# The first projection step as eight plain products, and an earlier load of the second step's weights

## The reference, cut to what matters

```python
def hybrid_layer(hid, norm_pre_w, w_in, ...):
    u = rms_norm(hid, norm_pre_w)                        # (2048, 1024)
    proj = jnp.einsum('bsd,de->bse', u, w_in)            # 6672 columns
    q, k, v, g_attn, z, xbc, dt_raw = jnp.split(proj, ...)
    attn = mixture_of_dilations(q, k, v) * silu(g_attn)
    y = ssd_chunked(silu(conv(xbc)), softplus(dt_raw + dt_bias), ...)   # and its gate and norm
    out = einsum(concat(attn, y), w_out)
    return hid + rms_norm(out, norm_post_w)
```

## Time and profile before

| | |
|---|---|
| time, median of 3 runs | 2194.11 us (2193.91 to 2195.1) |
| the profiled execution's own time | 2193.86 us |
| its span, first to last instruction | 2192.1 us |
| PE busy | 2131.7 us, 97% |
| opening (to the copy of dt's second part) | 0 to 54.78 us |
| steps 0 to 3, with the rounds | 54.87 to 136.55 us |

### The profile page before, as it was taken

The page is one execution under the profiler, slowest core; times in us unless marked ns, Lnnn a source line. Parts: engine busy times, 40 slices in busy tenths (PEclk is TensorE's granted clock), DMA queues, the critical chain, the costliest instruction groups (busy, mean ns, idle before and its releaser), DMA issues.

```text
span 2192.1 us, 34748 instructions
## 1 busy us (share of the span) xinstructions
PE 2131.7 (97%) x12009; PEld 1824.1 (83%) x12009; DVE 1374.5 (63%) x2581; ACT 1039.6 (47%) x2412; POOL 1443.0 (66%) x877
## 2 busy tenths in 40 slices
PE   6999999999999999999999999999997999999998
PEld 4778888888888887888889999999996788888877
DVE  7656666444556665363477777777777866766662
ACT  5334444343433443344357777777775622332231
POOL 5778888777678987777845564655642555655552
PEclk9999999999999999999999999999998899999999
DMA  4552333333623333343375656556547444434431
GB/s 152 198 182 88 111 109 116 115 97 122 224 94 99 96 125 106 109 122 97 115 168 127 155 135 145 120 146 155 135 110 250 153 140 145 139 125 135 135 104 58
DMA packets 261564, 288.23 MB, mean 131 GB/s; under 512 B 78516, under 2 KB 229232, under 8 KB 253328
## 3 DMA queue, kind: packets, MB, share of 16 engines
q1 hardware_dynamic: 260384, 278.68, 43.1%
q0 software_dynamic: 1008, 7.34, 0.8%
HBM read 195.80 MB, written 81.53 MB: 127 GB/s over the span
## 4 chain that ended last, share of the span: by engine, by line
PE 87%; DVE 4%; issue 3%; ACT 3%; DMA 2%; POOL 1%; SPq 0%; DVEq 0%; POOLq 0%; ACTq 0%
PE mm L1124 14%; PE mm L1126 14%; PE mm L1125 14%; PE ps_o L1885 9%; PE ps_t L1872 5%; PE ps_out L2481 5%; PE ps_out L2482 5%; PE ps_out L2488 5%; PE ps_s L1864 4%; PE ps_s L1865 3%; PE ps_y L2523 2%; PE turn L1226 2%; PE ps_state L2513 1%; PE ps_y L2504 1%; DMA tok_tile<-in_x_dram 1%
## 5 line engine op out<-in xcount | busy, mean ns | idle before, releaser
L1124 PE MATMUL mm<-b_hi,w_hi 128*128 128x512 f32 x1456 | 572.3, 393 | 8.3 <-DVE fm L902 6.5
L1126 PE MATMUL mm<-b_hi,w_lo 128*128 128x512 f32 x1456 | 567.9, 390 | 0.0
L1125 PE MATMUL mm<-b_lo,w_hi 128*128 128x512 f32 x1456 | 567.4, 390 | 0.0
L603 POOL TENSOR_TENSOR w_lo<-w_raw,w_hi 128x512 fp32r<-128x512 f32 x208 | 301.3, 1456 | 79.7 <-ACT w_hi L676 72.0
L1124 PEld LDWEIGHTS mm<-b_hi,w_hi 128*128 128x128 f32 x1456 | 273.9, 188 | 66.3 <-issue 10.4
L1126 PEld LDWEIGHTS mm<-b_hi,w_lo 128*128 128x128 f32 x1456 | 273.8, 188 | 57.6
L1125 PEld LDWEIGHTS mm<-b_lo,w_hi 128*128 128x128 f32 x1456 | 274.1, 188 | 55.6
L676 ACT ACTIVATE w_hi<-w_raw 128x512 fp32r<-128x512 f32 x208 | 130.8, 630 | 261.3 <-PE mm L1126 240.8
L1872 PE MATMUL ps_t<-ident_b,probs 128*128 128x128 f32 x1136 | 213.5, 278 | 6.3 <-ACT probs L1797 5.0
L902 DVE SCALAR_TENSOR_TENSOR fm<-mm,u 128x512 f32<-128x512 f32 x120 | 92.3, 769 | 181.9 <-PE mm L1126 181.7
L2481 PE MATMUL ps_out<-wo_hi,mix_hi 128*128 128x512 f32 x480 | 193.9, 404 | 1.3 <-ACT mix_hi L2374 1.3
(11 more groups left out here) (266 smaller groups left out, 4460.9 us busy)
## 6 DMA issues: line engine op xcount, KB each, us to landing
w_raw<-in_w_in_dram SPq DMA_DIRECT2D x52, 1024.0 KB, 5.3
feat<-fm SPq DMA_DIRECT2D x56, 512.0 KB, 5.0
tok<-tok_tile SPq DMA_DIRECT2D x52, 512.0 KB, 3.5
raw_q<-feat SPq DMA_DIRECT2D x32, 512.0 KB, 5.8
raw_k<-feat SPq DMA_DIRECT2D x32, 512.0 KB, 6.4
cum_b<-cum_scratch SPq DMA_DIRECT2D x16, 1024.0 KB, 7.5
cls_nat<-cls_out SPq DMA_DIRECT2D x64, 132.0 KB, 2.7
v_cls<-tok SPq DMA_DIRECT2D x64, 128.0 KB, 4.0
```

The lines of the kernel that those rows point to most:

```text
L603: pool.tensor_tensor(wl[o][:, :, :], source(o, n), wh[o][:, :, :].bitcast(F32), ALU.subtract)\
L1124: pe.matmul(bank, w_hi[:, k, :], bh[o][:, k, :], start=(opens and k == 0), stop=False)
L1125: pe.matmul(bank, w_hi[:, k, :], bl[o][:, k, :], start=False, stop=False)
L1126: last = pe.matmul(bank, w_lo[:, k, :], bh[o][:, k, :], start=False, stop=(closes and k == KH - 1))
```

## The change

Step 0 is no longer done by Strassen's scheme. Its outputs are A11 B11 + A12 B21, A21 B11 + A22 B21, and, since T1 = B12 - B11, A11 B11 + A11 T1 + A12 B22 and A21 B11 + A21 T1 + A22 B22: eight block products in six groups (`first_product`), of which four outputs are read by DVE (`first_read`) with two copies by ACT (`keep_first`). They stand among the transposes of the opening, which are reordered: B22 and T1 of all lanes first, then T3, T2, T4. POOL's block sums and three low parts of step 0 fall away. Of DVE's sums T2 is made in place. Weights of step 1 are loaded right behind the taps, where they used to wait for the last transpose; three tiles move to other rooms, so that this load has its room free. ACT makes the high part of A11 of step 1 ahead of the squares of round 0. Counts of semaphores follow (`products_before` and the like).

```diff
+FIRST_PRODUCTS, FIRST_READS, FIRST_PARTS, FIRST_COPIES = 6, 4, 4, 2
+A21 = S3
...
-        x_rooms = [*x_tok, x_wide[:, 0:D_MODEL], x_wide[:, D_MODEL:2 * D_MODEL]]
+        x_rooms = [*x_tok, place(nc, "x_lane2", SLOT_AT, [P, D_MODEL])[:, :],
+                   place(nc, "x_lane3", W_LO1_AT, [P, D_MODEL])[:, :]]
...
-        START_PARTS += [(o, j) for j in range(LANES) for o in (B22, T1, T3, T2, T4)]
+        START_PARTS += [(o, j) for j in range(LANES) for o in (B22, T1)]
+        START_PARTS += [(o, j) for j in range(LANES) for o in (T3, T2, T4)]
...
+            load_w(1)
             for i in range(HT, HT + 2):
-                sp.wait_ge(u_turned, GROUP_AT + 5 * (i - HT + 1))
+                sp.wait_ge(u_turned, PART_AT[T4, i - HT] + 1)
                 load_x(i)
-            sp.wait_ge(u_turned, START)
-            load_w(1)
...
-            sums(0)
-            low(0, 0)
-            token_sums(0)
+            pool.wait_ge(w_landed[0], 16)
+            low(A11, 0)
+            low(A12, 0)
+            token_sum(T1, 0)
+            low(A21, 0)
+            token_sum(T1, 1)
+            low(A22, 0)
             pool.wait_ge(dt_hi_made, 1)
...
+            def keep_first(o, seen, kept):
+
+                act.wait_ge(product, o)
+                act.activation(kept[:, :], seen[:, :], ACT.Copy, scale=steps[0].scale).then_inc(act_read, 1)
...
+                for r in range(GROUP_AT + 2 * j, GROUP_AT + 2 * j + 2):
+                    token_high(r, START_PARTS[r])
+                if j == 1:
+                    keep_first(1, mm[0], c1)
+                if j == 2:
+                    keep_first(3, mm[2], u2)
+            for j in range(LANES):
+                for r in range(SUMS_AT + 3 * j, SUMS_AT + 3 * j + 3):
                     token_high(r, START_PARTS[r])
                 if j == 0:
-                    high(5, 0)
-                    high(6, 0)
-                    read_first(steps[0])
-            read_dt_early()
+                    read_dt_early(0)
+            read_dt_early(1)
 
             for s in steps:
                 n = s.n
+                if n == 0:
+                    high(0, 1)
                 if n in PREP:
                     for half in range(2):
                         square(HT + 2 * PREP[n] + half)
...
-                for r in range(GROUP_AT + 5 * j, GROUP_AT + 5 * j + 5):
+                for r in range(GROUP_AT + 2 * j, GROUP_AT + 2 * j + 2):
                     token_low(r, START_PARTS[r])
+            first_read(2, 1, put(steps[0], 0, 0), mm[1], c1)
+            for j in range(LANES):
+                token_sums(j)
+                if j == 1:
+                    first_read(4, 2, put(steps[0], 1, 0), mm[0], u2)
+                for r in range(SUMS_AT + 3 * j, SUMS_AT + 3 * j + 3):
+                    token_low(r, START_PARTS[r])
+            first_read(5, 1, put(steps[0], 0, 1), mm[1], c1)
+            first_read(6, 2, put(steps[0], 1, 1), mm[2], u2)
...
                 if n == 0:
                     dve.wait_ge(u_turned, START)
-                else:
-                    dve.wait_ge(dve_read, READS * n)
+                    late_sums(PREP[n])
+                    continue
...
+            def first_product(bank, parts, *pairs):
+
+                pe.wait_ge(lo_made, parts)
+                for i, (w, o) in enumerate(pairs):
+                    last = dozen(bank[:, :], wh[w], wl[w], o, i == 0, i == len(pairs) - 1)
+                last.then_inc(product, 1)
...
             for j in range(LANES):
-                for r in range(GROUP_AT + 5 * j, GROUP_AT + 5 * j + 5):
+                for r in range(GROUP_AT + 2 * j, GROUP_AT + 2 * j + 2):
                     early_rows(r)
-                    if r == GROUP_AT:
-                        multiply(steps[0], 0)
                 if j == 0:
-                    pe.wait_ge(dt_lo_made, 1)
-                    dt_part(dt_banks[0], 0, B11, opens=True)
+                    pe.wait_ge(u_lo_made, GROUP_AT)
+                    first_product(mm[0], 1, (A11, B11))
                 elif j == 1:
-                    dt_part(dt_banks[0], 1, B21, closes=True).then_inc(dt_product, 1)
+                    first_product(mm[1], 2, (A12, B21))
+                    first_product(mm[2], 3, (A21, B11))
                 elif j == 2:
-                    dt_part(dt_banks[1], 0, B11, opens=True)
...
+                    pe.wait_ge(act_read, 1)
+                    first_product(mm[0], 4, (A22, B21))
+            pe.wait_ge(dt_lo_made, 1)
+            dt_part(mm[3], 0, B11, opens=True)
+            dt_part(mm[3], 1, B21, closes=True).then_inc(dt_product, 1)
+            for j in range(LANES):
+                for r in range(SUMS_AT + 3 * j, SUMS_AT + 3 * j + 3):
+                    early_rows(r)
+                if j == 1:
+                    pe.wait_ge(u_lo_made, SUMS_AT)
+                    pe.wait_ge(dve_read, 1)
+                    first_product(mm[1], 4, (A11, T1), (A12, B22))
+                elif j == 2:
+                    pe.wait_ge(act_read, 2)
+                    first_product(mm[2], 4, (A21, T1), (A22, B22))
+            pe.wait_ge(dt_read, 1)
+            dt_part(mm[3], 0, B11, opens=True)
+            dt_part(mm[3], 0, T1)
+            dt_part(mm[3], 1, B22, closes=True).then_inc(dt_product, 1)
...
             for s in steps:
                 n = s.n
-                for o in range(PRODUCTS):
-                    if n or o:
-                        multiply(s, o)
+                for o in range(PRODUCTS if n else 0):
+                    multiply(s, o)
```

More of the change, by code:

```diff
@@ L621, in gpsimd @@
                                dt_w[:, :, 0:SSM_HEADS].bitcast(F32), ALU.subtract).then_inc(dt_lo_made, 1)
[L622 to L631, removed]
+            token_sum(T1, 2)
+            token_sum(T3, 0)
+            token_sum(T1, 3)
+            for j in range(1, LANES):
+                token_sum(T3, j)
             for n in range(1, STEPS):
@@ L671, in high @@
                 act.wait_ge(w_landed[n % 2], 16 * (n // 2 + 1))
[L672 to L675, removed]
+                if n == 1:
+                    if o in (S2, S1, S4):
+                        act.wait_ge(u_turned, START)
+                    else:
+                        act.wait_ge(product, FIRST_PRODUCTS - 1 if o in (A11, A12) else FIRST_PRODUCTS)
+                elif n:
+                    act.wait_ge(product, products_before(n - 1) + o + 1)
+                if n and o in (S1, S2, S3, S4):
+                    act.wait_ge(sums_made, 4 * (n - 1) + {S1: 1, S2: 2, S3: 3, S4: 4}[o])
                 act.activation(wh[o][:, :, :], source(o, n), ACT.Copy).then_inc(hi_made, 1)
@@ L679, in square @@
                 act.wait_ge(rows_in[lane(i)], x_count(i))
-                act.activation(squares[:, :], x_room(i), ACT.Square, accum_out=sum_sq[:, i:i + 1])\
+                squares = u_tok[i] if i < LANES else early_squares if i < HT else half_tanh[:, :]
+                act.activation(squares, x_room(i), ACT.Square, accum_out=sum_sq[:, i:i + 1])\
                    .then_inc(squared, 1)
@@ L744, in reload, with read_dt_early @@
                     op = RELOAD[n, o]
-                    act.wait_ge(product, PRODUCTS * (TURN - 1) + op + 1)
+                    act.wait_ge(product, products_before(TURN - 1) + op + 1)
                     for j in range(LANES):
                         token_high(START + op * LANES + j, (op, j))
[L749 to L753, removed]
+            def read_dt_early(tb):
+                act.wait_ge(dt_product, tb + 1)
+                act.activation(dt_early_out[0:2 * SSM_HEADS, block_cols(tb)], mm[3][0:2 * SSM_HEADS, :], ACT.Copy)\
+                   .then_inc(dt_read, 1)
             def read_dt_late():
@@ L822, in scalar @@
                     read_first(s)
-                high(0, n + 1)
+                if n:
+                    high(0, n + 1)
                 for part in due(n, 0):
@@ L1093, in vector @@
                     cumulate()
[L1094 removed]
+                dve.wait_ge(dve_read, reads_before(n) + 3)
                 if s.conv:
@@ L1611, in gpsimd @@
             pool.memset(early.minus_half[:, :], -0.5).then_inc(S["made"], 1)
-            pool.wait_ge(first.product, PRODUCTS * LAST_STEP + S2 + 1)
+            pool.wait_ge(first.product, products_before(LAST_STEP) + S2 + 1)
             pool.memset(early.state[:, :, :], 0.0).then_inc(S["made"], 1)
```

165 lines of the change are left out of this document (86 added, 79 removed).

## The result

| | before | after |
|---|---|---|
| time, median of 5 runs each | 2194.11 us (2193.54 to 2195.1) | 2204.68 us (2202.88 to 2207.11) |
| the profiled execution's own time | 2193.86 us | 2205.18 us |
| its span | 2192.1 us | 2203.4 us |

The change makes the kernel slower: ratio 1.0048, 95% interval 1.0033 to 1.0063, 10.6 us by the medians. The forecast was 2204.3.

A forecast was written before the change was run, and what follows sets the result against it. The rounds, not PE, were taken to set the pace up to the end of step 3. 2193.86 + 11.5 (longer opening) - 1.1 (shorter round 0) = 2204.3 us, range 2198 to 2209.

The forecast's parts named there:

- Opening: PE before step 1: seven more products, product 1 at half clock and a 2.0 us stall make it 11.5 us longer.
- E: Start of ACT's copy of dt's second part, at the opening's end; forecast at 66.3 instead of 54.8.
- Round 0: ACT and DVE from the copy of dt to the store: 12.9 us instead of 14.0, 1.1 us gained.
- Steps 1 to 3: PE starts step 1 at 68.9, then waits about 12 us ahead of S1 (92.1); S4 at 100.8, not 90.4.
- The sum: Whole kernel: 2193.86 + 11.5 - 1.1 = 2204.3 us; this forecast was given 70%.
- The early load: Step 1's weights loaded ahead of tiles 8 and 9 in SP's queue; said to bring nothing.
- (a): Rival, faster: PE sets the pace, step 1 starts 3.4 us earlier; 2185 to 2190.5 us; chance 8%.
- (b): Rival, no change within 0.2%: opening grows by 5.6 only, round gains 2 or more; 2195 to 2198 us; chance 12%.
- (c): Rival, longer opening: a second half-clock stretch puts the copy of dt at 70 to 72; 2208 to 2210 us; chance 10%.

The follow-up runs named there:

- e4: The changed kernel with the load of step 1's weights put back behind the opening's last transpose; 2206.18 us, ratio 1.0054 to the kernel before.
- e5: The changed kernel with round 0's rows stored twice and SP waiting for both stores before loading round 1's tiles; 2207.23 us, ratio 1.0065.
- e1: The changed kernel with round 0 (squares, normalisations, late sums) moved into the opening; 2190.91 us, ratio 0.9987 to the kernel before.
- e7: e1 with round 0's late sums earlier, round 1's squares early, and step 0's outputs stored right behind the loads of round 1's tiles; 2188.89 us.
- e10: e7 with ACT's high part of A11 of step 1 put ahead of its copy of dt's second part; 2188.54 us, ratio 0.9978.
- e3: The kernel before, without the change, with rounds 0 and 1 moved early; 2188.92 us, ratio 0.9977, and 2187.81 us when run again.
- e11: e10 with SP's load of step 3's weights moved behind the loads of round 2's tiles; 2188.55 us, ratio 0.9978 to the kernel before.
- e2: e1 with round 1 moved early too (its squares and late sums); 2190.54 us, ratio 0.9985 to the kernel before.
- e12: e3 with SP's load of step 3's weights moved behind the loads of round 2's tiles; 2186.43 us, ratio 0.9968 to the kernel before.

## Why the prediction was right

**Opening: right.** Product 1 at 22.46 (22.8), at half clock to 27.73, which is 5.27 (5.1); one stall of 1.90 (2.0), at T2 of lane 1, where it was expected; no other gap up to 66.6; E at 66.69 (66.3), 11.9 behind before's 54.78. PE's timeline of after, beside the earlier trace rows:

```profile
22.46 0.78 PE L1182 MATMUL mm<-b_hi,w_hi 128*128 128x512 f32 x1
27.73 0.62 PE L1242 MATMUL turn<-ident,tok_tile 128*128 128x128 f32 x4
46.14 0.66 PE L1242 MATMUL turn<-ident,tok_tile 128*128 128x128 f32 x4 [1.90 <-DVE tok_tile L919]
69.26 0.80 PE L1182 MATMUL mm<-b_hi,w_hi 128*128 128x512 f32 x1 [2.40 <-POOL w_lo L630]
```

**Round 0: right, one term small.** The store came 12.3 behind E (78.96 less 66.69) for a forecast of 12.9: 1.7 gained, not 1.1. I had counted one normalisation as freed from POOL. Both were, as DVE's timeline of after shows beside the earlier trace rows, which gave 0.7 more. The way from the square to the first normalisation was 0.4 shorter too (67.70 to 69.46), and the four sums, as expected not freed, took 0.4 more (6.7; the first 1.60 for 1.18).

```profile
69.46 1.28 DVE L904 SCALAR_TENSOR_TENSOR tok_tile<-tok_tile,stat,fm 128x1024 f32<-128x1024 f32 x1
...
70.86 1.29 DVE L904 SCALAR_TENSOR_TENSOR tok_tile<-tok_tile,stat,fm 128x1024 f32<-128x1024 f32 x1
...
72.25 1.60 DVE L938 TENSOR_TENSOR conv_in<-tok_tile 128x512 f32<-128x512 f32 x1
```

**Steps 1 to 3: right in place, one size off without effect.** Step 1 began at 69.26 (68.9), S1 came at 92.05 (92.1), S4 at 100.49 (100.8). The wait ahead of S1 was 9.5 and not 12, since the four products ahead of it ran in part at half clock (0.79 granted from 69.0 to 76.4, behind the wait of 2.40), waited once more (0.38 at 76.74) and ended at 82.5 instead of 80. S1 did not move, for it follows ACT's copy; a wait that another engine ends takes up whatever PE is late. From S4 on the shift stayed as it was: 9.87 at S4 of step 2 (113.00 before, 122.87 after), 9.90 at P. PE's timeline of before:

```profile
113.00 0.47 PE L1124 MATMUL mm<-b_hi,w_hi 128*128 128x512 f32 x1 [2.76 <-DVE fm L902]
```

**The sum: right, by the place more than by the time.** 11.9 less 1.7 is 10.2, P moved by 9.90, the medians by 10.57, the two profiled runs by 11.3. The last 1.4 lie behind P, in the scatter. That the median was met within 0.4 is partly luck: the opening came out 0.4 longer than its term and the round 0.6 shorter, and the clock alone could have put E 1 us later, as in e4 and e5.

**The early load: wrong.** "It brings nothing" looked at PE's first need alone. The same load is what had POOL's sums done early, and with that made the normalisations short, which the text had counted one part before. e4 prices it: 1.3 us in the round, once its later opening is taken off.

**The rivals.** (a), PE setting the pace, gave 2185 to 2190.5 if round 1's tiles came in time. e1, e7 and e10 made them come, and ended at 2190.9, 2188.9 and 2188.5. So the price held as a time, but for 0.4 in e1, and the reason given for it did not: e3 has the same gain without one product moved. It came from freeing the rounds, and the 3.4 us of earlier start were waited for again at a later S4 (3.75 at S4 of step 2 in e10). (b) would have needed E near 60, which a first product at full clock was to give; it ran at half. (c) needed a second stretch at half clock in the opening; in after the matmuls follow at full clock from 28.55 on. In e4 and e5 such a stretch came, behind the stall of 1.90, and E was at 67.63 and 67.75: what (c) asked for does happen, but it put E 1 us later and not the 4 to 6 that (c) gave it.

## What to carry to other kernels

Before moving work into an engine's idle time, ask what starts when that stretch ends: 16 us of products left PE's path here, and a chain of stores and loads that began with the end of the opening was pushed back by nearly all that the opening had grown. Follow that chain from its first link to the point where the busy engine waits for it; as long as it is the longer one, work taken from the engine turns into waiting, and moving the chain's first link forward (e1: 13.5 us) is worth more than moving the work. Where whole times scatter by some us, compare a fixed point of the program's order just behind the edit; it is good to about one us here, where the rest of the span differs by 3.6. And take off first what differs ahead of the edit, as the clock did in e4.

## What was not expected of the hardware

**The same short wait ended in either clock.** Behind a wait of about 2.4 us at step 1's start PE went on at half clock in after and in e7 (first matmul's record 0.80 and 0.79 us) and at full clock in e1 (0.50, the next ones 0.23 apart). A wait of 2.76 ahead of S4 of step 2 was followed by full clock in before, and one of 2.47 in e11 by eight matmuls 0.43 apart. So with the opening's stall of 1.90: from 44 to 52 us PE was granted 1.00 in after, e1 and e7, and 0.79 in e2, e4, e5, e10 and e11. In the forecast I had looked for half clock only behind the long wait at S1. e3 and e12, whose waits were 1.33, 1.49 and 0.49, were granted 1.00 throughout 66 to 148.

**DVE's late sums are up to 2.6 times as long beside POOL.** In e10's opening, where POOL has nothing to do, each of the four takes 0.69 or 0.68 us; in step 1, beside POOL's low parts, 1.17 to 1.77:

```profile
53.64 0.68 DVE L948 TENSOR_TENSOR conv_in<-tok_tile 128x512 f32<-128x512 f32 x1
...
75.92 1.77 DVE L948 TENSOR_TENSOR conv_in<-tok_tile 128x512 f32<-128x512 f32 x1
```

The Trainium skill ("SBUF — State Buffer", Who interferes with whom) says that a DVE instruction with two inputs in SBUF contends with a GpSimd one that reads SBUF. The rows agree with it: POOL's low parts beside these sums took 1.73 to 1.74, and 1.29 to 1.30 alone. Which of the two waits for the other they don't show. It is a part of why each freed round still took its time: round 1's sums in e10 fill 74.83 to 81.1, right ahead of the store.
